# Retention scale from a bound, and another order of the copies in an attention stage on one Trainium2 core

## What is computed

```python
def _retention(rq, rk, rv, rg, logit_f, logit_b, s0_f, s0_b, gn):
    y_f, s_f = _retention_dir(rq, rk, rv, logit_f, s0_f)
    y_b, s_b = _retention_dir(jnp.flip(rq, 1), jnp.flip(rk, 1), jnp.flip(rv, 1), logit_b, s0_b)
    y = y_f + jnp.flip(y_b, 1)
    mu = jnp.mean(y, axis=-1, keepdims=True)
    var = jnp.mean(jnp.square(y - mu), axis=-1, keepdims=True)
    y = ((y - mu) * lax.rsqrt(var + EPS)).astype(rv.dtype)
    B, T = y.shape[0], y.shape[1]
    y = y.reshape(B, T, MIX_B) * gn
    return jax.nn.silu(rg) * y, s_f, s_b

def _merge(attn, ret, ga, gb, w_up_a, w_up_b, w_o):
    return (jax.nn.sigmoid(ga) * (attn @ w_up_a) + jax.nn.sigmoid(gb) * (ret @ w_up_b)) @ w_o
```

## Time and profile before

| | |
|---|---|
| median of 3 runs | 2368.84 us (2360.94 to 2376.19) |
| the profiled execution | 2369.24 us, span 2367.4 us, 33503 instructions |
| PE busy | 2202.3 us, 93% |
| DVE busy | 1813.7 us, 77% |
| ACT busy | 1252.1 us, 53% |
| POOL busy | 431.1 us, 18% |

### The profile page before, as it was taken

One profiled execution on the slowest core, in us unless ns is written; L12 is line 12 of the kernel. 1 busy time (PEld: TensorE's weight loads), 2 busy tenths in 40 slices (PEclk: granted clock), 3 DMA queues, 4 the chain that ended last, 5 costly groups with the idle time before them and its releaser, 6 DMA issues. The chain is left out here.

```text
span 2367.4 us, 33503 instructions
## 1 busy us (share of the span) xinstructions
PE 2202.3 (93%) x11984; PEld 1196.6 (51%) x11984; DVE 1813.7 (77%) x3803; ACT 1252.1 (53%) x1675; POOL 431.1 (18%) x395
## 2 busy tenths in 40 slices
PE   6899898898688999999999999989999999999997
PEld 3566666444355665444555554544444444444443
DVE  2575543545677666789999999963899999999999
ACT  1465572324566853553444445766665556555663
POOL 0011110000011120022323232420122222222220
PEclk9799999899799999999999999999999999999999
DMA  9665562000466765478899989996877877787771
GB/s 390 236 213 166 183 229 90 18 18 9 166 236 206 280 223 184 160 244 266 285 347 308 347 303 342 323 358 232 321 290 291 316 288 294 288 316 288 292 283 71
DMA packets 192073, 574.28 MB, mean 243 GB/s; under 512 B 18464, under 2 KB 52032, under 8 KB 184256
## 3 DMA queue, kind: packets, MB, share of 16 engines
q1 hardware_dynamic: 113872, 329.69, 40.4%
q0 software_dynamic: 47104, 167.80, 19.1%
q10 hardware_dynamic: 30960, 75.07, 8.2%
HBM read 455.48 MB, written 117.00 MB: 242 GB/s over the span
## 5 line engine op out<-in xcount | busy, mean ns | idle before, releaser
L297 PE MATMUL u_ps<-h_hi,lin_hi 128*128 128x512 f16 x1024 | 389.9, 381 | 5.7 <-PEq L74 5.7
L297 PE MATMUL u_ps<-h_lo,lin_hi 128*128 128x512 f16 x1024 | 389.8, 381 | 0.0
L297 PE MATMUL u_ps<-h_hi,lin_lo 128*128 128x512 f16 x1024 | 389.6, 380 | 0.0
L279 DVE SCALAR_TENSOR_TENSOR lin_lo<-lin_raw,lin_wsc,lin_hi 128x1024 f16<-128x1024 f32 x132 | 169.4, 1284 | 162.0 <-ACT lin_hi L273 161.6
L1927 POOL DMA_INDIRECT row<-v_dram,picked x128 | 179.1, 1400 | 578.6 <-DVE acc L2562 449.8
L1992 POOL DMA_INDIRECT row<-u_rows_dram,picked x128 | 176.0, 1375 | 518.3 <-DVE dot_junk L2176 354.0
L273 ACT ACTIVATE lin_hi<-lin_raw,lin_wsc 128x1024 f16<-128x1024 f32 x132 | 151.1, 1146 | 191.9 <-DVE lin_wsc L138 142.3
L2433 PE MATMUL ps_w<-oh_turned,oh_buf 128*128 128x128 f16 x1024 | 224.3, 219 | 4.4 <-ACT region L2105 4.4
L2673 PE MATMUL y_ps<-region 128*128 128x512 f16 x512 | 194.0, 379 | 1.4 <-PEq L1931 1.4
L2675 PE MATMUL y_ps<-region 128*128 128x512 f16 x512 | 194.0, 379 | 0.0
L2675 PE MATMUL y_ps<-lin_hi,lin_raw 128*128 128x512 f16 x512 | 194.0, 379 | 0.0
(11 more groups left out here) (405 smaller groups left out, 4447.4 us busy)
## 6 DMA issues: line engine op xcount, KB each, us to landing
lin_raw<-w_all_dram SPq DMA_DIRECT2D x132, 512.0 KB
act_scratch<-activated ACTq DMA_DIRECT2D x128, 256.0 KB
wgt_scratch<-region ACTq DMA_DIRECT2D x64, 512.0 KB
region<-v_dram SPq DMA_DIRECT2D x15, 2048.0 KB
oh_buf<-v_dram SPq DMA_DIRECT2D x15, 2048.0 KB
proj<-w_mod_dram SPq DMA_DIRECT2D x16, 1536.0 KB, 14.6
act_buf<-w_all_dram SPq DMA_DIRECT2D x38, 512.0 KB, 5.1
lin_hi<-split_scratch SPq DMA_DIRECT2D x64, 256.0 KB
```

The source lines that it names most:

```text
L279: nc.vector.scalar_tensor_tensor(out=self.lo[b][:], in0=self.raw[b][:], scalar=self.wsc[:, self.col(b)], in1=self.hi[b][:], op0=ALU.mult, ...
L297: last = nc.tensor.matmul(self.ps[b % 2][:, half, 0:ts.stop - ts.start], w_[:, kc, :], x_[:, kc, ts], start=(j == 0 and kc == 0), stop=(j ...
```

## The change

- **Retention scale.** The scale no longer comes from the squares of the finished heads. Since the square of a normalised element is at most 128, the squares of the gates (`silu(rg)`, four ACT instructions in unit 3), times 128 times the squared norm weights (two small DVE instructions in unit 4), bound the sum. PE sums it in unit 4, DVE makes the scale in unit 5. So ACT copies each head's high half at slot 3 of the unit that finishes it, where the square stood, and DVE makes the low half (`ret_low`) at slot 0 of the next unit; head 3's low half stays behind the loop.
- **Normalisation chain.** Its first four instructions become three (`scalar_tensor_tensor` with -0.5 and 1.5 folded in).
- **Halves of the pairs.** `high` moves from slot 4 of the even unit to slot 1 of the next, `low` from slot 0 to slot 2 of that unit, ahead of the normalisation chain.
- **End.** The squares' totals and scales of the first merge weights move from slots 1 to 4 of unit 9 to slots 0, 2 and 3; the first weight's high half (`lin.head`) and `take(9)` go into slots 2 and 3.
- **Start.** `take(0)` moves behind `ksteps`' exponent and `decays(0)`; the DVE does the first two of unit 3's eight maxima ahead of the `lgw` chain.
- Four load semaphores at the program's start are merged into two, and each scale's waits with them; the loads and their order stay. POOL clears two more dead semaphores.

```diff
@@ ACT, ahead of the loop
                         negate(2)
-                        take(0)
                         act.wait_ge(s("kst_mul"), 1)
                         nc.scalar.activation(ksteps[:], ksteps[:], ACT.Exp).then_inc(s("kst_exp"), 1)
                         act.wait_ge(s("lg_done"), 1)
                         act.wait_ge(s("ret_ld"), 16 * 9)
                         decays(0)
+                        take(0)
@@ ACT, body(u, k, i)
+                            if u == UNITS - 1 and k == 2:
+                                act.wait_ge(s("ret_av"), PIECES)
+                                act.wait_ge(s("ret_st"), RH)
+                                lin.head(act, Q_UP, 0)
+                            if u == UNITS - 1 and k == 3:
+                                take(u)
                             if k == 3 and 0 <= h < RH:
+                                act.wait_ge(s("ret_scaled"), 1)
                                 act.wait_ge(s("ret_out"), h + 1)
-                                nc.scalar.activation(h_lo[:, RH + h, :].bitcast(BF16), y_t[:, h, :], ACT.Square,
-                                                     accum_out=hsum[:, 2, h:h + 1]).then_inc(s("ret_hsq"), 1)
-                            if k == 4 and u % 2 == 0:
+                                nc.scalar.activation(h_hi[:, RH + h, :], y_t[:, h, :], ACT.Copy, scale=hscale[:, 2:3]
+                                                     ).then_inc(s("ret_hi"), 1)
+                            if u == CTX + 1 and k < RH:
+                                act.wait_ge(s("silu_g"), k + 1)
+                                nc.scalar.activation(h_lo[:, RH + k, :].bitcast(BF16), proj[:, M_RG + k, :], ACT.Square,
+                                                     accum_out=hsum[:, 2, k:k + 1]).then_inc(s("ret_gsq"), 1)
+                            if k == 1 and u % 2:
                                 high(u // 2 - 1)
@@ DVE, ahead of the loop
                         act_scale(dve, link, 1, pr[:, 400:400 + NALL // P], "att_scaled")
+                        maximum(3, 0)
+                        maximum(3, 1)
                         dve.wait_ge(s("lg_exp"), 1)
...
-                        for part in range(8):
+                        for part in range(2, 8):
                             maximum(3, part)
@@ DVE, body(u, k, i)
-                            elif k == 0:
+                            elif k == 2:
                                 low(u // 2 - 1)
+                            if u == CTX + 2 and k == 0:
+                                gamma = cols[:, C_GN:C_GN + RH]
+                                link(V.scalar_tensor_tensor(out=hsum[:, 2, RH:2 * RH], in0=gamma, scalar=float(DK), in1=gamma,
+                                                            op0=ALU.mult, op1=ALU.mult))
+                                dve.wait_ge(s("ret_gsq"), RH)
+                                V.tensor_tensor(hsum[:, 2, 0:RH], hsum[:, 2, 0:RH], hsum[:, 2, RH:2 * RH], ALU.mult
+                                                ).then_inc(s("ret_bound"), 1)
+                            if u == CTX + 3 and k == 0:
+                                dve.wait_ge(s("ret_total"), 1)
+                                act_scale(dve, link, 2, pr[:, 400:400 + RH], "ret_scaled")
                             if k == 2 and 0 <= h < RH:
                                 dve.wait_ge(s("gn_root"), h + 1)
-                                link(V.tensor_tensor(t, root, root, ALU.mult))
+                                link(V.scalar_tensor_tensor(out=t, in0=root, scalar=-0.5, in1=root, op0=ALU.mult, op1=ALU.mult))
                                 link(V.tensor_tensor(t, t, var, ALU.mult))
-                                link(V.tensor_scalar(t, t, -0.5, 1.5, ALU.mult, ALU.add))
-                                link(V.tensor_tensor(r, root, t, ALU.mult))
+                                link(V.scalar_tensor_tensor(out=r, in0=t, scalar=1.5, in1=root, op0=ALU.add, op1=ALU.mult))
...
+                            h = u - CTX - 5
+                            if k == 0 and 0 <= h < RH:
+                                ret_low(h)
-                            if u == UNITS - 1 and k in (2, 4):
-                                lin.scale(dve, Q_UP, k // 2 - 1)
+                            if u == UNITS - 1 and k in (0, 3):
+                                lin.scale(dve, Q_UP, k // 3)
@@ PE, rows(u) and body(u, k, i)
+                            if u == CTX + 4:
+                                pe.wait_ge(s("ret_scaled"), 1)
...
+                            if u == CTX + 2 and k == 4:
+                                pe.wait_ge(s("qrow"), u + 2)
+                                total_pe(pe, "ret", pr[:, 400:400 + RH], 2, RH, "bound", 1)
-                            if u == UNITS - 1 and k in (1, 3):
-                                if k == 1:
+                            if u == UNITS - 1 and k in (0, 2):
+                                if k == 0:
                                     pe.wait_ge(s("qrow"), UNITS)
                                 lin.total(pe, Q_UP, k // 2)
```

More of the change, by code:

```diff
@@ L604, in norm_act, with total_pe @@
                         copy(kc)
-            def total_pe(pe, tag, total, k, n, of="hsq"):
-                pe.wait_ge(s(f"{tag}_{of}"), n)
+            def total_pe(pe, tag, total, k, n, of="hsq", count=None):
+                pe.wait_ge(s(f"{tag}_{of}"), count or n)
                 nc.tensor.matmul(total, ones[:], hsum[:, k, 0:n], start=True, stop=True).then_inc(s(tag + "_total"), 1)
@@ L706, in _ @@
                     def _(sp):
-                        for dst, name in ((cvec[:], "cvec"), (bmod[:], "bmod"), (cols[:], "cols"),
-                                          (pick_c[:], "pick_c"), (ones[:], "ones"), (x_t[:], "x_t"), (ident[:], "ident")):
-                            sp.dma_start(dst, a[name]).then_inc(s("ld_" + name), 16)
+                        for dst, name, of in ((cvec[:], "cvec", "cvec"), (bmod[:], "bmod", "cols"), (cols[:], "cols", "cols"),
+                                              (pick_c[:], "pick_c", "picks"), (ones[:], "ones", "picks"), (x_t[:], "x_t", "x_t"),
+                                              (ident[:], "ident", "ident")):
+                            sp.dma_start(dst, a[name]).then_inc(s("ld_" + of), 16)
                         for i in range(NMW):
@@ L851, in _ @@
                         dve.wait_ge(s("parts_used"), NMW)
[L852 to L853 removed]
+                        dve.wait_ge(s("ld_cols"), 32)
                         for g in (0, 1):
@@ L980, in _ @@
                         pe.wait_ge(s("csil"), 1)
-                        pe.wait_ge(s("ld_pick_c"), 16)
-                        pe.wait_ge(s("ld_ones"), 16)
+                        pe.wait_ge(s("ld_picks"), 32)
                         def gather(i):
@@ L1256, in _ @@
                         slots(body)
[L1257 to L1263, removed]
-                                                 ).then_inc(s("ret_hi"), 1)
                         high(UNITS // 2 - 1)
@@ L1318, in query_decays, with ret_low @@
                                                 ).then_inc(s("qdec"), 1)
+                        def ret_low(h):
+                            dve.wait_ge(s("ret_hi"), h + 1)
+                            V.scalar_tensor_tensor(out=h_lo[:, RH + h, :], in0=y_t[:, h, :], scalar=hscale[:, 2:3],
+                                                   in1=h_hi[:, RH + h, :], op0=ALU.mult, op1=ALU.subtract
+                                                   ).then_inc(s("ret_lo"), 1)
                         def mask(i):
@@ L1442, in _ @@
                         normalise(last)
-                        for h in range(RH):
-                            dve.wait_ge(s("ret_hi"), h + 1)
-                            V.scalar_tensor_tensor(out=h_lo[:, RH + h, :], in0=y_t[:, h, :], scalar=hscale[:, 2:3],
-                                                   in1=h_hi[:, RH + h, :], op0=ALU.mult, op1=ALU.subtract
-                                                   ).then_inc(s("ret_lo"), 1)
+                        ret_low(RH - 1)
                         dve.wait_ge(s("a_mm"), key_at(UNITS))
@@ L1624, in _ @@
                         slots(body)
-                        pe.wait_ge(s("qrow"), UNITS)
-                        pe.wait_ge(lin.sem("scaled", 1), Q_UP + 1)
-                        total_pe(pe, "ret", pr[:, 400:400 + RH], 2, RH)
                     @block.gpsimd
```

2 lines of the change are left out of this document (removed).

## The result

The median of six runs is 2346.29 us (2342.84 to 2351.76), beside 2367.78 us for the kernel before in the same comparison (six runs, 2356.78 to 2376.19). The ratio is 0.9914, 95% interval 0.9898 to 0.993: a gain of 21.5 us, inside the range forecast (2344 to 2361), 5.7 us under the time forecast (2352), and short of 1% (23.7 us). The profiled execution took 2344.24 us.

A forecast was written before the change was run, and what follows sets the result against it. PE's waits for exponents at unit openings, the slow clock behind them and DVE's tail were taken as the bound; terms -8.3 - 4.1 - 1.5 + 0.5 - 4.4 + 1.2 = -16.6 gave 2352.0 us, range 2344 to 2361.

The forecast's parts named there:

- start: Block's start: early maxima delay the decay-logit chain, `decays(0)` ahead of `take(0)` takes some back; +1.2 us, ends -0.7 and +1.6.
- opening of unit 3: Unit 3's first attend: without the merge's copy ahead it starts 6.7 us earlier, 1.6 of slow clock returns; -8.3 us.
- opening of unit 5: Unit 5's first attend: the 2.44 us idle goes, and 1.69 of slow clock with it; -4.1 us.
- tail: DVE's chain behind the loop, ahead of the merge: 17.44 us becomes 13.0; -4.4 us, ends -2.5 and -5.8.
- Openings of 7, 8 and 9: Units 7 to 9: copy leaves the path, chain shortens, `low(2)` costs some; sum -1.5 us, ends 0 and -4.
- more of the clock: Rival: all six openings yield as unit 5 does, total -23 us, time 2345 and less; chance 0.11.
- so DVE just covers: Unit 3: DVE frees the bank at 444.51 plus 0.49, PE reaches its second pair of maxima at about 445.
- The rival in which DVE takes ACT's place: Unit 3: PE needs DVE a slot sooner, the unit yields 4 us less, the clock falls again; 2358 us, chance 0.10.
- The copy as holder: Openings: the merge's copy on ACT holds up PE's exponent; the rival that it doesn't gave 2364 us, chance 0.03.
- a bound of 14 for "wrong": Tail: more than 14 us from the variance's root to the last `low` would show the forecast wrong.
- Fused instructions: Normalisation chain: fusing costs 0.07 us each; the rival at half rate, 6.2 us on the path, gave 2358, chance 0.01.
- The rival in which it stays there for longer: Merge: PE stays at the lower clock longer, each 2 us costing 1; slower by over 1% (2393 us), chance 0.02.

The follow-up runs named there:

- the delayed trace of the kernel after: The kernel after with eight extra small DVE instructions that nothing reads, delaying the attention block's start: one run 2350.33 us, block 222.6.
- the second trace of before: The kernel before, run again unchanged: one run 2370.42 us, block 243.0.
- the halves alone: The kernel before with only `high` moved to slot 1 and `low` to slot 2 of the odd unit: 2357.43 us against 2367.73, ratio 0.9965.
- two experiments with 13.45: Kernel after with pair halves, `take(0)` and early maxima put back: 2363.18 us; kernel after without early maxima, pair halves in slot 0 of units 7 and 9: 2347.99.
- the bound and the end alone: The kernel after with the halves of the pairs, `take(0)` and the two early maxima put back: 2363.18 us against 2367.73, ratio 0.9981.

## Why the prediction was right where it was, and what it missed

| step | forecast, us | measured in the traces, us |
|---|---|---|
| start | +1.2 | +1.2 (34.56 to 35.79) |
| unit 2, clock behind its 2.33 wait | not in the sum | -2.3: clock 3.0, new wait for DVE +0.7 |
| opening of unit 3 | -8.3 | -7.3: idle 6.3, clock 1.6, new wait of 0.28 and what stands behind it +0.6 |
| extra product in unit 4 | +0.2 | +0.1 |
| opening of unit 5 | -4.1 | -4.2 |
| unit 6, clock behind its 1.88 wait | not in the sum | -1.7 |
| opening of unit 7 | -0.8 | -0.8, and -1.7 of clock not in the sum |
| `low` in front of the chain, unit 8 | +0.3 | +0.4 |
| unit 9: opening; its totals | -1.0; +0.3 | -1.1; +0.4 |
| tail | -4.4 | -4.9 |
| sum | -16.6 | -21.9 |

**The sum.** The mechanisms that the sum has, and their places, held, and their sizes to 1.0 us each; the median fell into the range and within 1% of before. The block gave 5.3 us more than forecast, and the table names them: 2.3 + 1.7 + 1.7 = 5.7 us at units 2, 6 and 7, less 0.4 in the other rows. The term that was mis-sized stands in "Openings of 7, 8 and 9": it gives a reason to count no clock at unit 9, which was right (3.19 us of wait, and it fell), and none at unit 7, where 1.7 came. For units 2 and 6 there was no term, since no instruction at them moved. The prediction read each loss of clock in the trace of before as a fixed consequence of the wait in front of it. The runs show that for a wait of this size it isn't. The rival "more of the clock" had this mechanism, with 0.11 and -23: it came true at units 6 and 7 and not at unit 9, and the rest of the -22 came at unit 2, which is no opening. The range held because it was wide enough for 5.3 us that the sum did not see. With the lower clock at units 6 and 7, as in the delayed trace of the kernel after, the block would have gained 18.5 (21.9 less twice 1.7, an estimate from these rows).

The rows of units 2 and 3 hang together. In the second trace of before, unit 2 took 18.4 us in place of 20.0, and the wait at unit 3 was 8.17 in place of 6.94: there DVE's `normalise` sets when the unit opens, and what PE gains ahead of it turns into waiting. Only their sum, -9.6 for a forecast -8.3, can be compared safely.

**Unit 3** gave 1.0 less than forecast. DVE was early enough, as forecast ("so DVE just covers"), save for 0.28. The exponent was later than forecast, with 0.62 idle left, because `take(2)` stands behind the query decays of head 0 on ACT: these end at 431.13 (430.42 + 0.71), 0.6 behind unit 2's last attend on PE (429.53 + 1.02), and the copy starts at 431.15. Before, ACT was through with them 0.4 ahead of that attend's end, and the forecast took this over. The rival in which DVE takes ACT's place fell: no wait of 3 to 4 us for DVE stands in unit 3.

**The copy as holder** is shown by the halves alone. That rival is out.

**Tail.** From the root to the last low half it takes 12.6 us (ACT ends the root at 583.85, DVE ends at 596.43), against 13.0 forecast and a bound of 14 for "wrong". The scale was quicker, and so was the low half of the pair. Of the 14.57 from variance to merge 1.1 are the price of `high(3)` and `low(3)` behind the root, as two experiments with 13.45 show.

**Fused instructions.** The two fused ones of the chain take 0.82 us each and the plain one between them 0.83. The page Vector Engine (DVE) Microarchitecture Reference of the Trainium skill, "Points that are easy to get wrong", has them at half throughput. This trace doesn't agree, nor does that of before, where the fused row took 0.89 beside 0.83, and the measurement decides.

**Start.** +1.2 came out to the tenth in the first trace, and +1.6 to +1.7 in the two others of the kernel after (36.17 and 36.23), so the tenth is luck. PE restarts 25.1 us behind the block's first product in place of 21.8, 3.3 later (3.4 forecast), has two maxima fewer behind that, and `decays(0)` ahead of `take(0)` took `kdec`'s wait off. The experiment without the early maxima splits it: moving the decays alone gives -1.0 (34.56 to 33.55), the early maxima +2.2. What speaks for the early maxima is that unit 2's clock held in every trace with them. From the block's first product to unit 3's first attend it still takes 56.0 to 56.4 us with them and 53.9, 54.3 and 57.2 without, so no net gain is shown.

**The merge** still opens at the lower clock, and comes back after less time than before: PE waits 9.30 us ahead of it (10.57 before), its pairs of products take 0.69 to 0.74 us until about 600.4, 3.7 us in, and then 0.43; before this took 5.7 us. The rival in which it stays there for longer is out.

What stays open is which property of the program's course sets whether a 2 us wait costs the clock, and so why the kernel after kept it at units 2, 6 and 7 in all three of its traces and the kernel before in neither of its two. The traces show waits of one length both ways, mostly the same way for one program, but not always.

## What to carry to other kernels

An in-order engine that serves several consumers should do the copy that nobody wants soon behind the one that the next engine waits for: look for a long wait whose releaser was itself waiting, and ask what stood in front. Such a wait was paid twice on PE, once idle and, when the clock fell behind it, once more. When a change moves a block in time, give the clock losses behind its short waits a range of their own, both ways, also where no instruction moves; and test a small gain inside the block, since in the whole kernel's time it drowns.

## What the runs showed of the chip that was not expected

- A wait of 1.88 us on PE at unit 6, with the same instructions before and behind it, is followed by the lower clock level (1.2 GHz) in six traces and by the full one (2.4 GHz) in six others: attend 0 to attend 1 takes 5.6 to 5.7 us or 4.0. The ten traces whose chip is on record come from three chips, and each of these shows both outcomes, so the chip alone doesn't decide it. A wait of 1.74 at unit 7 goes both ways too (5.4 to 5.5 us or 3.8). One of 2.33 at unit 2 held with the early maxima and fell without them. At unit 5 one of 2.44 fell (5.7 to 7.0 us in three traces of the kernel before) and one of 2.22 held (4.0 with the bound and the end alone). Waits of 3.19 us and more at the openings, 16 in twelve traces, were always followed by the lower level.
- The fall needn't come at once: in one trace the first attend behind the wait took 1.12 us, the full level, and the score behind it 1.58.
- Shortening the start by 2.2 us left the block as long as it was, because units 7 and 8 opened at the lower clock. A local gain can be given back in later stretches that the edit doesn't touch.
